# State blocks ahead of merge gates, prompt gates in column strips, six zero products at the start

## What is computed

```
P = rmsnorm(x) @ w_in            # HGRN2 q,f,i,g | NSA q | K,V x3 | NSA gates (24) | two merge gates
a = HGRN2(...)                   # recurrent state per head, 128 x 128
b = NSA(...): g = sigmoid(ngate) # o = g0*o_cmp + g1*o_slc + g2*o_win
x += (sigmoid(g_a)*(a W_a) + sigmoid(g_b)*(b W_b)) @ w_out
x += W_down(gelu(conv3(h2 W_gate)) * (h2 W_up))
```

## Time and profile before

| | us |
|---|---|
| median of 3 timed runs | 1176.08 |
| the 3 runs | 1176.12, 1176.08, 1165.91 |
| profiled execution, its own time | 1166.02 |
| its span, first to last instruction | 1164.2 |
| PE busy in the span | 1142.0 (98%) |
| DVE, ACT, POOL busy | 707.1, 544.1, 173.2 |
| mean granted clock of PE | 0.996 |

### The profile page before, as it was taken

How to read it: one execution, slowest core, us unless ns; L and a number is a source line. 1 busy time by engine, 2 the same in 40 slices (tenths; PEclk the granted TensorE clock), 3 DMA queues, 4 the chain that set the end, 5 groups by cost and what they waited for, 6 DMA issues and landing times.

```text
span 1164.2 us, 21121 instructions
## 1 busy us (share of the span) xinstructions
PE 1142.0 (98%) x8613; PEld 1032.4 (89%) x8613; DVE 707.1 (61%) x1302; ACT 544.1 (47%) x867; POOL 173.2 (15%) x300
## 2 busy tenths in 40 slices
PE   6999999999999999999999999999999999999997
PEld 5987776778999999999999787676899999999997
DVE  5686265457567777763558644545756677776442
ACT  4532275653355555542454234755435555554231
POOL 1154300013110100100105450000312110010000
PEclk9999999999999999999999999999999999999998
DMA  9555332347644444324456525213784444432501
GB/s 292 164 150 190 107 99 73 109 119 219 223 153 134 158 157 155 123 93 160 145 133 212 165 86 167 73 40 119 220 266 154 137 157 151 145 109 91 178 29 46
DMA packets 151498, 165.99 MB, mean 143 GB/s; under 512 B 31492, under 2 KB 114214, under 8 KB 151078
## 3 DMA queue, kind: packets, MB, share of 16 engines
q1 hardware_dynamic: 151402, 164.64, 45.3%
HBM read 156.22 MB, written 12.46 MB: 145 GB/s over the span
## 4 chain that ended last, share of the span: by engine, by line
PE 94%; DVE 2%; DMA 1%; ACT 1%; issue 0%; SPq 0%; DVEq 0%; ACTq 0%
PE mm L671 66%; PE ax L671 23%; PE ax L674 5%; DMA ring<-in_state_hgrn 1%; ACT mixb L1325 1%; DMA attb<-in_norm_final 0%; DVE ring_low L1681 0%; DVE mixb L1831 0%; DVE mixb L2096 0%; DVE work_parts L2065 0%; PE mm L674 0%; DVE mixb L1848 0%; DVE mixb L2097 0%; DVE merged_low L2065 0%; DVE mixb L2250 0%
## 5 line engine op out<-in xcount | busy, mean ns | idle before, releaser
L671 PE MATMUL mm<-work_parts 128*128 128x320 f32 (+2 forms) x1120 | 356.5, 318 | 1.1 <-DVE h_low L1675 1.1
L1681 DVE TENSOR_TENSOR ring_low<-ring,work_parts 128x2048 fp32r<-128x2048 f32 (+2 forms) x116 | 256.0, 2207 | 125.4 <-ACT work_parts L1325 124.7
L671 PE MATMUL mm<-h_low,work_parts 128*128 128x320 f32 x1024 | 319.3, 312 | 0.0
L671 PE MATMUL mm<-work_parts,ring_low 128*128 128x320 f32 x1024 | 315.6, 308 | 0.0
L1325 ACT ACTIVATE work_parts<-ring 128x2048 fp32r<-128x2048 f32 (+2 forms) x116 | 211.9, 1827 | 159.7 <-PE mm L671 90.3
L671 PEld LDWEIGHTS mm<-work_parts 128*128 128x128 f32 (+1 forms) x1120 | 209.2, 187 | 9.2 <-issue 2.0
L671 PEld LDWEIGHTS mm<-h_low,work_parts 128*128 128x128 f32 x1024 | 193.0, 188 | 0.3
L671 PEld LDWEIGHTS mm<-work_parts,ring_low 128*128 128x128 f32 x1024 | 193.1, 189 | 0.0
L671 PE MATMUL ax<-act_parts,work_parts 128*128 128x320 f32 x544 | 127.2, 312 | 0.6 <-DVE ring L2087 0.6
L671 PE MATMUL mm<-act_parts,work_parts 128*128 128x320 f32 x480 | 117.4, 310 | 0.3 <-DVE merged_low L2065 0.3
L671 PE MATMUL mm<-hT,ring 128*128 128x320 f32 x384 | 109.6, 437 | 0.0
(11 more groups left out here) (235 smaller groups left out, 1584.7 us busy)
## 6 DMA issues: line engine op xcount, KB each, us to landing
ring<-in_w_gate_up SPq DMA_DIRECT2D x44, 1024.0 KB, 7.0
ring<-in_w_in SPq DMA_DIRECT2D x10, 2048.0 KB, 8.5
ring<-in_w_in SPq DMA_DIRECT2D x18, 1024.0 KB, 5.7
ring<-in_w_down SPq DMA_DIRECT2D x8, 1536.0 KB, 6.7
ring<-in_w_out SPq DMA_DIRECT2D x4, 2048.0 KB, 13.9
ring<-in_w_down SPq DMA_DIRECT2D x4, 2048.0 KB, 8.1
ring<-in_w_in SPq DMA_DIRECT2D x32, 128.0 KB, 3.1
ring<-in_cache_cmp_kv SPq DMA_DIRECT2D x32, 128.0 KB
```

The lines of the kernel that those rows point to most:

```text
L671: return nc.tensor.matmul(out, lhsT, rhs, start=start, stop=stop)
L1681: V.tensor_tensor(unit_of(u, ring_r), unit_of(u, ring), unit_high(u).bitcast(F32), ALU.subtract).then_inc(*st.up(w_low[l]))
```

## The change

1. `BLOCKS`: st1 stands before mg2. ov5 now loads st1 and mgb3 loads mg2. At st1's turn SP now stores the states, waits for them and loads br1; at mg2's turn it waits for mgb5 and loads wo0.
2. The prompt's gates leave `compressed_rows`. `prompt_gates` makes them with the 32 last columns of w_kvc stationary and 256 tokens moving, eight plain products into four 32-partition strips of one bank. ACT copies the bank, and `prompt_gates_turned` sums the strips and turns them with two products against `gsum` (four shifted identities, summed by DVE at the start); ACT then applies one sigmoid.
3. In DVE's order `unit_turned(0)` goes ahead of `unit_scale(1)`.
4. DVE clears one tile of hT at the start, and PE makes six plain products of it, into a bank that nobody reads, ahead of the input's turns.

```diff
-           "st0", "mg2", "st1", "br0", "mg3", "br1", "wo0", "wo1"] + [f"ff{n}" for n in range(NJ // JPB)]
+           "st0", "st1", "mg2", "br0", "mg3", "br1", "wo0", "wo1"] + [f"ff{n}" for n in range(NJ // JPB)]
...
+    out += [("kvc0", "A"), ("kvc1", "A"), ("gtf", "A"), ("kvc2", "A")]
...
-    out += [("cp", "A"), ("hidk", "A"), ("hidv", "A"), ("gsel0", "V"), ("gsel1", "V")]
+    out += [("cp", "A"), ("gtt", "A"), ("hidk", "A"), ("hidv", "A"), ("gsel0", "V"), ("gsel1", "V")]
...
-                for k in range(KD if i < 2 else 0):
-                    last = mm(bank[0:TM[i], 256:280], hT[:, k, P * i:P * i + TM[i]], w[:, k, 256:280], k == 0,
-                              k == KD - 1)
                 last.then_inc(mm_full[L], 1)
+
+            def prompt_gates():
+
+                w = kt_of("w_kvc", KD, 280)
+                bank = begin(MM[L], "gtf")
+                for k in range(KD):
+                    strip = slice(32 * (k % 4), 32 * (k % 4) + 32)
+                    last = mm(bank[strip, 0:SEQ], w[:, k, 248:280], hT[:, k, 0:SEQ], k < 4, k >= 4)
+                last.then_inc(mm_full[L], 1)
+
+            def prompt_gates_turned():
+
+                bank = begin(AXR[L], "gtt")
+                pe.wait_ge(*MM[L].emptied_at("gtf"))
+                for i in range(2):
+                    last = mm(bank[:, 24 * i:24 * i + 24], gtF[:, P * i:P * i + P], gsum[:, :], True, True)
+                last.then_inc(ax_full[L], 1)
...
                 compressed_rows(1, l)
+                prompt_gates()
...
                 compressed_rows(2, l)
+                prompt_gates_turned()
...
+            pe.wait_ge(zeros_ready, 1)
+            for n in range(6):
+                mm(mmb[3][:, 0:T], hT[:, 0, 0:P], hT[:, 0, :], True, True)
             pe.wait_ge(first_consts_in, 16)
...
-                        A(gts[:, i, :], bank[:, 256:280], ACT.Sigmoid)
...
+                        bank = take(MM[L], "gtf")
+                        A(gtF, bank[:, 0:SEQ], ACT.Copy).then_inc(*st.up(mm_act[L]))
...
+                bank = take(AXR[L], "gtt")
+                A(gts[:, 0:2, :], bank[:, 0:48].rearrange("p (i c) -> p i c", i=2), ACT.Sigmoid).then_inc(
+                    *st.up(ax_act[L]))
...
+            V.memset(hT[:, 0, :], 0.0).then_inc(zeros_ready, 1)
             V.memset(epsb[:, :], EPS).then_inc(eps_ready, 1)
...
+            link(V.tensor_tensor(gsum[:, :], ident[:, 8:32], ident[:, 40:64], ALU.add))
+            link(V.tensor_tensor(gsum[:, :], gsum[:, :], ident[:, 72:96], ALU.add))
+            link(V.tensor_tensor(gsum[:, :], gsum[:, :], ident[:, 104:128], ALU.add))
...
                 unit_scale(0)
+                unit_turned(0)
                 unit_scale(1)
-                unit_turned(0)
```

More of the change, by code:

```diff
@@ L116, in mm_plan @@
     out = [("par", "V")] + [(f"hf{h}", "V") for h in range(HH)] + [(f"hq{h}", "V") for h in range(HH)]
-    out += [(f"nq{m}", "V") for m in range(4)] + [(f"{x}{i}", "A") for x in ("hi", "kvn", "kvc") for i in range(3)]
+    out += [(f"nq{m}", "V") for m in range(4)] + [(f"{x}{i}", "A") for x in ("hi", "kvn") for i in range(3)]
+    out += [("kvc0", "A"), ("kvc1", "A"), ("gtf", "A"), ("kvc2", "A")]
     out += [(f"hg{h}", "V") for h in range(HH)]
@@ L267, in hybrid_step @@
         ctok = work[:, 6280:7048].rearrange("p (i c) -> p i c", i=3)
+        gtF = work[:, 7048:7048 + SEQ]
+        gsum = sb("gsum", 24)
         kvT = work[:, 7048:9096].rearrange("p (w b t) -> p w b t", w=2, b=4)
@@ L398, in hybrid_step @@
         end_rs_ready, eps_ready = sem("end_rs_ready"), sem("eps_ready")
-        spare, half_read = sem("spare"), sem("first_half_read")
+        spare, half_read, zeros_ready = sem("spare"), sem("first_half_read"), sem("zeros_ready")
         first_consts_in, consts_in, copied = sem("first_consts_in"), sem("consts_in"), sem("window_copied")
```

## The result

| | before | after |
|---|---|---|
| median, us | 1172.15 (8 runs, 1165.91 to 1176.12) | 1179.61 (8 runs, 1178.58 to 1182.28) |
| ratio of the medians' runs | | 1.0069, 95% interval 1.0048 to 1.0090 |
| profiled execution, span | 1166.02, 1164.2 | 1178.58, 1176.8 |
| mean granted clock | 0.996 | 0.981 |

The changed kernel is 0.7% slower. That is within 1%, and 1179.6 lies inside the forecast range.

A forecast was written before the change was run, and what follows sets the result against it. PE's instructions and its few waits were taken to bound the kernel. +6.6 + 4.0 - 3.9 + 0.4 - 0.8 = +6.3 us on the profiled 1166.0 gave 1172.3 us, range 1161 to 1184.

The forecast's parts named there:

- PE waits for mg2: Ahead of gate 4, mg2 lands at about 253.9 and is split late; 3.3 us lost a layer, +6.6 us.
- clock behind that wait: At gate 4, the granted clock falls after PE stands 4.6 us; 2.0 us a layer, +4.0 us.
- gates in strips: Prompt's gates: 3.48 us of narrow products go, strips (1.1) and turn (0.44) come; -3.9 us over two layers.
- DVE order: PE's wait for the turned tile moves one step, to values(0); +0.4 us for two layers.
- start: Ahead of the first weight product, faster input turns leave w_hf's landing at 13.5 as what is late; -0.8 us.
- The base of the sum: The terms were added to the profiled execution's 1166.0 us, 10.1 below the median of the runs shown.
- Rival 1: At gate 4, PE waits for mg2 but the clock stays up: 1168.3 us; chance 0.23.
- Rivals 2: mg2 comes early enough to lose little, the clock stays up, the start keeps its clock: 1161.1 us; chance 0.12.
- rival 3: br0 shares the DMA engines with mg2, each layer losing up to 11 us: 1187.7 us; chance 0.07.
- upper kind: Whole kernel: slower executions, 10.1 us above the profiled one; the forecast would then be 1182.4 us.
- rival 4: Prompt's gates: strips don't run side by side, 3.46 for 1.1 us, +4.7: 1177.0 us; chance 0.08.
- the cover of br1: br1, asked for later, lands by 296.6, before ACT first asks at 297.14; costs nothing, thin in that worst case.

The follow-up runs named there:

- The repeated runs: The kernel before, unchanged, timed and profiled again: 1168.8 us (12 runs), beside 29 more executions with a median of 1172.62.
- The run with the later decay: Changed kernel with POOL's first decay of the sample states put behind DVE's split of mg2's first unit: 1177.76 us, ratio 1.0074 to the kernel before.
- the blocks alone: Kernel before with st1 ahead of mg2 in the list of blocks, nothing else: 1182.24 us, ratio 1.0085.
- work in the wait: Changed kernel with ten plain products of constants while PE stands for mg2: 1175.0 us, ratio 1.0057 to the kernel before.
- halves: Plain products of two head gates cut in halves, eight instructions of each moved earlier; on the kernel before 1171.73 us, with gates in strips 1165.29 us.
- the strips alone: Kernel before with the prompt gates in strips; blocks, DVE order and start as before: 1172.58 us, ratio 1.0003.
- without the swapped blocks: Changed kernel with mg2 ahead of st1 again, its other three edits kept: 1170.32 us, ratio 0.9983 to the kernel before.

## Why the forecast was wrong, and where it was right

The terms, on the two profiled executions (1178.58 - 1166.02 = 12.6 us), by the distance between the same instructions in both traces:

| step | forecast | measured |
|---|---|---|
| PE waits for mg2 | +6.6 | +9.3 (4.7 and 4.6) |
| clock behind that wait | +4.0 | +5.3 (2.7 and 2.6) |
| gates in strips | -3.9 | -3.4 (1.7 each) |
| clock behind the gates | no term | +2.8 (1.5 and 1.3) |
| DVE order | +0.4 | +0.4 |
| start | -0.8 | 0 |
| end of the kernel | no term | -1.5 |

They sum to 12.9; 0.3 us are not assigned.

**The base of the sum** failed first. I wrote that the median lay 10.1 us above the profiled execution and that no row shows what separates them, and then made the forecast from the profiled one. The repeated runs show what separates them: the granted clock, 0.997 to 0.986 over the executions of one unchanged program. The profiled one, with 0.996 and the earlier trace rows at 1.00 in mid-kernel, was one of the fastest. The changed kernel has its falls in all eight runs (0.980 to 0.981, of which the reading at the start takes 0.004), so against the median (1172.15) it loses 7.5 us and against the profiled execution 12.6. The sum of +6.3 on the later median would have given 1178.4, near what came, but by luck: the terms were too small by 6.3 us, and the median already holds part of the falls.

**The wait for mg2: mechanism right, size off.** The order of requests, the landing (254.3 for 253.9) and ACT's split came as forecast. The step that failed is the 2.28 us of DVE's split, taken from the earlier trace rows as if it came out the same beside other work; it makes 1.08 of the 1.4 us that gate 4 starts later than forecast in layer 0. In the kernel before POOL's decay of the states begins at 255.16, behind that split; the earlier st1 lets it begin at 253.70, in front of it, and the split takes 3.36. The run with the later decay shows that this is the cause. By the Trainium skill (SBUF — State Buffer, SBUF: two separate sides) a DVE instruction with two SBUF inputs and a GpSimd instruction that reads SBUF exclude each other for a whole instruction. The trace agrees: POOL's second decay ends at 253.70 + 3.78 = 257.48, 1.21 us behind the split's start, and the split is 1.08 longer. In layer 1, with the blocks alone and with work in the wait it is the same: in all six splits that began beside a decay, the split is longer by what was left of the decay (0.98 to 1.48 us) less 0.13 or 0.14. The trace of the kernel before already held such a case: another split of this size, at 55.50, took 3.94 us beside a POOL instruction that ended at 57.30 (1.80 left, 1.66 longer). I had followed what queues behind the wait, and had not asked what the earlier st1 sets off on POOL.

**The clock behind the wait** fell as forecast, and with work in the wait it did not. Its price was too small: 2.0 was taken for 24 products, but the clock stayed at 0.50 for some six us of gate 4, which cost 2.7. The row of 24 was misread. Only the first 16 of its products start 0.267 us apart (up to 23.79); the last eight are 0.15 apart. Gate 4 has 22 at 0.267, each 0.12 us dearer. Rival 1 (the clock stays up) is out. Rivals 2 and 3 are out with the landing time. (One number of rival 3 was wrong: mg2 landing 3 us a layer later gives 1178.3 and not more than 1187.8; only an execution of the upper kind, at 1182.4, would have got there.)

**The gates.** The strips run side by side: 1.0 us, 1.1 forecast, so rival 4 is out. The two changes of tiling mode show no idle of their own in PE's timeline (120.87 to 121.87 for 16 instructions, `nqr0` right behind). What failed is that the sum ended there. The next 30 us hold turns, one-column products and products of 15 columns between wider ones, and there the clock falls in every layer that was profiled with strips and without halves: near 131 and 152 with the strips alone, near 130 without the swapped blocks, near 150 in the changed kernel. Without strips it falls there in half of the layers, so the strips made likelier what happens anyway. That the 3.5 us of products taken away ahead of this stretch are what tips it is argued from this count and from the runs with halves, not shown by itself; no run tells it from a rival, that the strip products put in their place do it. I looked for a fall only where PE would stand. In the strips' fall at 131 PE is busy 5.00 of 5.00 us.

**The start.** The turns took 4.62 us and not the 2.9 that I had from a later row, w_hf was in at 14.16 and not at 13.5, the parameters at 15.94, behind the upper bound of 15.5. From 12 us on the clock was at 0.81 and 0.50, so the first products ran as slowly as before. The gain of 0.8 went into two waits for DMAs.

**The DVE order** was right in size and place, and so was the cover of br1: no wait for a branch block is in PE's list.

## What to carry to other kernels

Before a sum is set on a profiled execution, its mean clock has to be set beside that of the timed ones; the spread of an unchanged kernel tells how much is to be lost or won there. Taking work off a busy PE paid here only where the stretch behind it still held the clock up: 1.7 us a layer came and went within the same layer, and in the two kernels with strips that also had half of a dense group of products moved between small ones, no fall was seen in that stretch and the kernel was 0.3 to 0.4% faster than before. When a load is moved earlier, follow everything that its landing releases, on engines off the path too.

## What the runs showed of the hardware that was not expected

- The granted clock fell with PE busy all the time by the profile, in which the ends of matmuls are modelled (5.00 of 5.00 us at 0.66 from 131 to 136 with the strips alone; 12.00 of 12.00 at 0.52 from 1152 on). In the 6 us ahead of the first PE had done turns, products of 140 columns and one-column products; in the second it does turns and one-column sums.
- Whether it falls in such a stretch differs between executions of one program: 1.00 from 150 to 153 in one execution of the kernel before, 0.66 from 151 to 156 in another. The Trainium skill (TensorE: Matmul & The Clock Gate, What's actually happening) says of the start of a kernel that the number of slow products there varies between runs of the same kernel. Here the like is seen in mid-kernel, in 41 executions from 1166.1 to 1177.4 us.
- A DVE instruction of 2.28 us took 3.12 to 3.63 when it began while a POOL instruction of 1.89 ran, longer by what was left of that one less 0.13 or 0.14 in six of six cases, and 2.29 again when the POOL instruction came later.
- Products of a cleared tile do raise the clock: the turns behind them took 4.62 us instead of 7.35.
